# Second block's down product by one level of Strassen's algorithm, with its sums on VectorE

## Chip, core and metric

The kernel runs on one core of one Trainium2 chip, in f32 throughout. The metric is the device time of one execution in microseconds, taken as the median of several runs. A profiled execution of the same program gives the trace; its own time stands beside its span below. The engines are TensorE (PE; PEld are its weight loads), VectorE (DVE), ScalarE (ACT), GpSimd (POOL) and SyncE (SP), which here only issues transfers.

## What is computed

Two transformer blocks one after the other on 512 tokens of width 1024. The first has latent attention, a state-space branch, cross-attention and a mixture of 64 experts; the second has gated mixing, sparse attention and a feed-forward layer. The change is in the last lines of the second block:

```python
D_FF = int(math.ceil(8 * D_MODEL / 3 / 256)) * 256      # 2816
...
        h = rmsnorm(x, norm_ffn_w[l])
        x = x + (jax.nn.silu(h @ w_gate[l]) * (h @ w_up[l])) @ w_down[l]
    return rmsnorm(x, final_norm_w)
```

The down product multiplies activations of 512 x 2816 with weights of 2816 x 1024.

## The kernel before

Each engine has one program, written out by hand in the order in which it runs; engines meet through semaphores that count up (`wait_ge`). The matrix products land in eight PSUM banks of 128 x 512 f32. A fixed list (`psum_order`, line 157) names every bank tile in order, who reads it (act or dve), and the class `Plan` works out which bank it gets and which earlier tile must have been read first (`free`). `OWN_BANKS` (line 108) gives "fd", the down product, its eight banks in turn.

Weights of the dense products come as panels of 128 x 1024 f32 (512 KB) from the array `stream` into `ring`, twelve slots in on-chip memory. `panel_plan` (line 315) lists them in order and says after which event a slot may be filled again; SP issues them in `load_panel` (line 830) and waits there for the event. The weights of the experts come from other arrays, by larger transfers, partly into the same ring.

The stage before the down product computes gate and up, 22 units (`for n in range(UNITS)`, lines 1534 on TensorE, 1964 on ScalarE, 2721 on VectorE). Each unit is already one level of Strassen's algorithm in Winograd's form: seven block products p1 to p7 of four matmuls each (128 x 128 by 128 x 256), in turn over the eight banks (`unit_product`, line 1523, bank (7n + part) mod 8), four sums of weights for each unit on VectorE (`weight_sums`, line 2692, `sums_ready`), and seven additions on VectorE that put the parts together (`unit_read` counts them). After each odd unit VectorE multiplies silu(gate) by up, which makes two of the 22 feature blocks `actf[k]` (128 features x 512 tokens) ready and counts `actf_ready`.

The down product (`down_step`, line 1555) multiplies those blocks with panels of w_down. Half 0 (the first 512 output columns) runs over all 22 blocks with the four token tiles inside, in four banks; half 1 runs tile after tile, each over all 22 blocks. VectorE adds each finished bank to the residual x4. In half 1 it then takes the tile's mean square (`ask_rms`, line 2111), GpSimd raises it to the power -0.5, VectorE scales the tile, and SP stores it.

Of the kernel before, what the change touches and what calls it, by code (L numbers as in the profile page):

```python
# [107 lines left out]
OWN_BANKS = {"s5y": (7,), "s2": (0, 1, 2, 3), "pt2": (4, 5), "o2": (6, 7), "fd": (2, 3, 4, 5, 6, 7, 0, 1)}  # L108
# [48 lines left out]
def psum_order():  # L157
# [151 lines left out]
    for i in range(8):  # L309
        add("fd", i, "dve")  # L310
# [4 lines left out]
def panel_plan():  # L315
# [34 lines left out]
    p += [("fd", k, ("fd", 4 * (k // 11) + 3) if k % 11 == 10 else ("ffn", k - k // 11)) for k in range(FT)]  # L350
# [6 lines left out]
def host_stream(w):  # L357
# [7 lines left out]
    def rows(m, k, c0, n):  # L365
        return m[k * P:(k + 1) * P, c0:c0 + n]

    def two(m, i, c0, n=512):
        out = np.zeros((P, 2, 512), f)
        for b in range(2):  # L370
            out[:, b, :n] = rows(m, 2 * i + b, c0, n)
        return out.reshape(P, 1024)
# [28 lines left out]
    def pair(m, i, n):  # L401
# [18 lines left out]
        "fd": lambda i: two(w["w_down_2"][0], i % 11, 512 * (i // 11)),  # L420
# [102 lines left out]
def build(nc, a, out, scratch):  # L523

    plan = Plan(psum_order(), 8)
    with ExitStack() as ctx:
# [215 lines left out]
        outb = slab1  # L742

# [82 lines left out]
        def _(sp):  # L826
# [3 lines left out]
            def load_panel(n):  # L830

                if n >= RING:
# [3 lines left out]
                    elif n - N1 >= RING:  # L836
# [3 lines left out]
                        elif key[0] == "ffn":  # L840
                            sp.wait_ge(ffn_used, key[1] + 1)
                        else:
# [103 lines left out]
        def _(pe):  # L946
# [608 lines left out]
            def down_step(half, t, k):  # L1555
                return nc.tensor.matmul(tile("fd", 4 * half + t)[:, :], actf[k][:, t * P:(t + 1) * P],  # L1556
                                        panel("fd", 11 * half + k // 2)[:, (k % 2) * 512:(k % 2) * 512 + 512],
                                        start=(k == 0), stop=(k == FT - 1))

            for t in range(NT):  # L1560
                free("fd", t)
            pe.wait_ge(unit_kept, UNITS)
            pe.wait_ge(unit_read, 7 * UNITS - 2)
            for k in range(FT):
                if k % 2 == 0:
                    need("fd", k // 2)
                    pe.wait_ge(actf_ready, k // 2 + 1)
                for t in range(NT):
                    mm = down_step(0, t, k)
                    if k == FT - 1:  # L1570
                        close(mm, "fd", t)
                    elif k % 2 == 1 and t == NT - 1:
                        mm.then_inc(ffn_used, 1)
            for t in range(NT):
                free("fd", 4 + t)
                if t == 0:
                    pe.wait_ge(unit_read, 7 * UNITS)
                for k in range(FT):
# [1407 lines left out]
```

## Time and profile before

| | us |
|---|---|
| median of three runs | 2114.28 |
| lowest and highest | 2112.44, 2119.64 |
| the profiled execution's own time | 2117.95 |
| its span | 2116.1 |
| mean granted TensorE clock | 0.976 of full |

The span runs from the first to the last instruction of the trace; the execution's own time has 1.85 us more around it. Busy time is that of an engine's instructions. TensorE's records overlap, so the mean duration of one is longer than what it costs; its rate is busy time divided by count. Each f32 matmul leaves two records. "Idle before" is time in which an engine stood still just before instructions of the group, with what ended it. A line number can be that of a helper: L1997 is any VectorE addition, subtraction or product of two tensors, L2000 any scaled one.

### The profile page before, as it was taken

Reading aid. Unit: us, or ns where it says so; the run is one execution under the profiler, and the core shown is the slowest. Engines: PE = TensorE matmul, PEld = TensorE weight load, DVE = VectorE, ACT = ScalarE, POOL = GpSimd, SP = SyncE. Lnnn points to the kernel's source line nnn. Section 1 sums busy time; section 2 is a strip of 40 time slices with the busy share of each in tenths; the row PEclk is TensorE's granted clock in tenths of the full one; section 3 lists DMA queues with packets and bytes.
Section 4 is the critical chain, followed back from the end, with each engine's and each line's share of the span. In section 5 each row is a group of like instructions: output and inputs, shape, how many; then the busy total and the mean of one; then the engine's idle time right before and its main releaser. Section 6 shows DMA issues by size and latency. Waiting matters only on the chain.

```text
span 2116.1 us, 26992 instructions
## 1 busy us (share of the span) xinstructions
PE 1955.6 (92%) x10450; PEld 1021.1 (48%) x10450; DVE 891.8 (42%) x1804; ACT 474.3 (22%) x1042; POOL 336.2 (16%) x295
## 2 busy tenths in 40 slices
PE   7897999999997899999989998799988899999997
PEld 3333434444543344443333333344745588888443
DVE  5998691213167323332332234601266555454012
ACT  2233531010121233333323332211236000000000
POOL 0654161000006401101010015300023000000000
PEclk9998999999999999999999999899999999999999
DMA  6116743220415999999999999603310122222200
GB/s 233 50 47 206 208 134 148 80 70 23 159 60 216 316 393 400 400 399 393 386 388 382 388 391 373 240 20 139 140 40 2 40 80 100 80 83 97 80 30 30
DMA packets 74730, 393.68 MB, mean 186 GB/s; under 512 B 12194, under 2 KB 12450, under 8 KB 57760
## 3 DMA queue, kind: packets, MB, share of 16 engines
q1 hardware_dynamic: 45216, 300.95, 37.8%
q10 hardware_dynamic: 16592, 58.01, 8.1%
q0 software_dynamic: 12848, 33.74, 4.4%
q8 instruction: 47, 0.77, 0.2%
q14 instruction: 27, 0.22, 0.0%
HBM read 371.51 MB, written 55.09 MB: 202 GB/s over the span
## 4 chain that ended last, share of the span: by engine, by line
PE 70%; DMA 14%; DVE 9%; issue 4%; POOL 2%; ACT 1%; SPq 0%; POOLq 0%; ACTq 0%; DVEq 0%
PE bank L975 28%; PE bank L1306 13%; PE bank L1531 13%; DMA ring<-w_exp_down 10%; PE bank L1556 6%; PE bank L984 2%; DVE slab L2000 1%; DMA slab<-w_exp_down 1%; DVE work L1994 1%; PE bank L1324 1%; DVE s5x L1997 1%; DMA slab<-x_rows,s5x 1%; DVE slab L1997 1%; PE bank L1382 1%; PE bank L1037 1%
## 5 line engine op out<-in xcount | busy, mean ns | idle before, releaser
L975 PE MATMUL bank<-slab,ring 128*128 128x512 f32 (+1 forms) x784 | 330.1, 581 | 12.0 <-DMA ring<-stream 11.1
L975 PE MATMUL bank<-ring,slab 128*128 128x512 f32 (+1 forms) x608 | 252.8, 577 | 3.7 <-ACT slab L1594 1.9
L2458 DVE COPY slab<-bank 32x512 f32<-32x512 f32 x124 | 80.9, 688 | 410.9 <-PE bank L1314 410.9
L1306 PE MATMUL bank<-ring,slab 128*32 128x512 f32 x1536 | 232.7, 607 | 19.7 <-DMA slab<-w_exp_down 16.4
L1306 PE MATMUL bank<-slab 128*32 128x512 f32 x1536 | 227.9, 597 | 21.9 <-DMA ring<-w_exp_down 14.6
L975 PEld LDWEIGHTS bank<-slab,ring 128*128 128x128 f32 x784 | 149.0, 192 | 188.7 <-issue 187.1
L1314 PE MATMUL bank<-ring,slab 128*32 128x512 f32 x512 | 227.4, 598 | 0.0
L1314 PE MATMUL bank<-slab 128*32 128x512 f32 x480 | 214.4, 600 | 0.0
L975 PEld LDWEIGHTS bank<-ring,slab 128*128 128x128 f32 x608 | 115.7, 191 | 137.3 <-issue 129.5
L2774 POOL TENSOR_TENSOR small<-small 128x1 f32<-128x1 f32 (+2 forms) x30 | 26.6, 888 | 873.9 <-DVE small L1994 873.9
L1556 PE MATMUL bank<-ring,slab 128*128 128x512 f32 x352 | 151.2, 593 | 0.0
L1306 PEld LDWEIGHTS bank<-ring,slab 128*32 128x32 f32 x1536 | 73.1, 112 | 153.3 <-issue 153.2
L1306 PEld LDWEIGHTS bank<-slab 128*32 128x32 f32 x1536 | 71.2, 110 | 152.4 <-issue 145.9
L2849 POOL DMA_INDIRECT slab<-x_rows,s5x x64 | 61.9, 967 | 503.6 <-PE bank L1268 494.4
L1531 PE MATMUL bank<-work,s5x 128*128 128x256 f32 x528 | 117.6, 379 | 0.0
L1997 DVE TENSOR_TENSOR slab<-bank,slab 96x256 f32<-96x256 f32 (+2 forms) x98 | 49.3, 505 | 151.2 <-PE bank L1556 132.7
L1556 PEld LDWEIGHTS bank<-ring,slab 128*128 128x128 f32 x352 | 67.0, 190 | 83.6 <-issue 83.6
L1531 PEld LDWEIGHTS bank<-work,s5x 128*128 128x128 f32 x528 | 100.5, 190 | 13.4
L1997 DVE TENSOR_TENSOR work<-bank,work 128x256 f32<-128x256 f32 (+1 forms) x74 | 33.5, 454 | 164.5 <-PE bank L975 89.9
L1821 ACT ACTIVATE slab<-bank 32x512 f32<-32x512 f32 x124 | 66.6, 584 | 106.9 <-PE bank L1314 106.9
L1777 ACT ACTIVATE slab<-bank 128x384 f32<-128x384 f32 x128 | 55.8, 488 | 141.3 <-DVE slab L2425 120.9
L1531 PE MATMUL bank<-slab,ring 128*128 128x256 f32 x352 | 79.7, 380 | 0.8 <-DVE slab L1994 0.8
(302 smaller groups left out, 2581.8 us busy)
## 6 DMA issues: line engine op xcount, KB each, us to landing
ring<-stream SPq DMA_DIRECT2D x171, 512.0 KB, 4.3
slab<-w_exp_gu SPq DMA_DIRECT2D x32, 2048.0 KB, 25.2
ring<-w_exp_gu SPq DMA_DIRECT2D x32, 2048.0 KB, 23.5
ring<-w_exp_down SPq DMA_DIRECT2D x32, 1024.0 KB, 28.5
slab<-w_exp_down SPq DMA_DIRECT2D x32, 1024.0 KB, 28.0
y_rows<-zeros ACTq DMA_DIRECT2D x1, 24960.0 KB, 127.7
y_rows<-slab ACTq DMA_DIRECT2D x64, 384.0 KB, 10.4
gb<-rows ACTq DMA_DIRECT2D x5, 512.0 KB, 5.3
```

Source lines behind the costliest of these rows:

```text
L975: mm = nc.tensor.matmul(dst, lhs[k], rhs[k], start=(k == 0), stop=(k == len(lhs) - 1))
L984: mm = nc.tensor.transpose(tile(name, i)[0:parts, j * P:(j + 1) * P], x, ident)
L1306: mm = nc.tensor.matmul(g_bank[32 * g:32 * g + 32, :], x[:, k, 32 * g:32 * g + 32], w[:, 512 * k:512 * k + 512], start=(k == 0), stop=(k = ...
L1314: mm = nc.tensor.matmul(bank[2 + 3 * t + half][96:128, :], h[:, c * CAP + 32 * t:c * CAP + 32 * t + 32], d[:, c * D + 512 * half:c * D + 5 ...
L1531: mm = nc.tensor.matmul(unit_bank(n, p), w[:, k * P:(k + 1) * P], x[:, k, :], start=(k == 0), stop=(k == 3))
L1556: return nc.tensor.matmul(tile("fd", 4 * half + t)[:, :], actf[k][:, t * P:(t + 1) * P], panel("fd", 11 * half + k // 2)[:, (k % 2) * 512: ...
L1777: i = nc.scalar.activation(xe[b][:, 4 * j:4 * j + 4, :], bank[j][:, 0:4 * CAP].rearrange("p (k n) -> p k n", n=CAP), ACT.Copy)
L1821: i = nc.scalar.activation(ye[b % 2][0:32, 512 * half:512 * half + 512], bank[2 + half][96:128, :], ACT.Copy)
L1997: return nc.vector.tensor_tensor(out_, x, y, op)
L2458: i = nc.vector.tensor_copy(ye[b % 2][32:64, 512 * half:512 * half + 512], bank[5 + half][96:128, :])
L2774: nc.gpsimd.tensor_tensor(rstd[:, at:at + w], var[:, at:at + w], minus_half[:, 0:w], ALU.pow).then_inc(rstd_ready, 1)
L2849: pool.indirect_dma_start(xg[e % 2][0:CAP, :], None, scratch["x2"], bass.IndirectOffsetOnAxis(ap=slot_tok[:, e:e + 1].bitcast(U32), axis=0 ...
```

## The change

The activations A (512 tokens x 2816 features) and the weights W (2816 x 1024) are each cut into two by two blocks. Tokens are cut into two halves of 256, output columns into two of 512, and features by turns: block row k of the eleven takes `actf[2k]` as the first and `actf[2k+1]` as the second. Seven products replace eight: p1 = A11 W11, p2 = A12 W21, p5 = S1 T1, p6 = S2 T2, p7 = S3 T3, p3 = S4 W22, p4 = A22 T4, where S1 = A21 + A22, S2 = S1 - A11, S3 = A11 - A21, S4 = A12 - S2 are 256 wide and T1 = W12 - W11, T2 = W22 - T1, T3 = W22 - W12, T4 = W21 - T2 are 512 wide. Each product has two token tiles and eleven contraction blocks.

TensorE makes three passes. The first has p1, p2 (plain steps) and, one block behind, p6, p7 (sum steps), in all eight banks. The second has p5 and p3 by turns. The third has p4, tile after tile. VectorE makes the eight sums of each block from the ring during the first pass (`down_sums`); S2, T2, S3 and T3 have two places each, so it waits for `ffn_used` before it writes a third; S1, T1, S4 and T4 are kept for all eleven blocks in memory that is free by then. ScalarE copies p1 out of its banks. VectorE adds the other parts to x4 as they close; tiles 0 and 1 are finished after p3, tiles 2 and 3 after p4.

The panels of w_down are ordered by pairs for each block (W11 with W21, then W12 with W22), and six more panels, "fb", bring W22 a second time for the second pass: 28 in place of 22. A slot that held a "fd" panel is refilled once TensorE has used the block's sums and VectorE has made all eight.

```diff
@@ -105,7 +105,10 @@
-OWN_BANKS = {"s5y": (7,), "s2": (0, 1, 2, 3), "pt2": (4, 5), "o2": (6, 7), "fd": (2, 3, 4, 5, 6, 7, 0, 1)}
+OWN_BANKS = {"s5y": (7,), "s2": (0, 1, 2, 3), "pt2": (4, 5), "o2": (6, 7), "fd": (2, 3, 4, 6, 5, 7, 0, 1)}
+DOWN_PARTS = ("p1", "p2", "p6", "p7", "p5", "p3", "p4")
...
-    for i in range(8):
-        add("fd", i, "dve")
+    for p in DOWN_PARTS:
+        for t in range(2):
+            add("fd", 2 * DOWN_PARTS.index(p) + t, "act" if p == "p1" else "dve")
...
-    p += [("fd", k, ("fd", 4 * (k // 11) + 3) if k % 11 == 10 else ("ffn", k - k // 11)) for k in range(FT)]
+    p += [("fd", i, ("ffn", i // 2)) for i in range(FT)]
+    p += [("fb", i, ("fd", 2 * DOWN_PARTS.index("p3") + 1)) for i in range(FT // 4 + 1)]
...
+        KH = FT // 2
+        def a_block(i, j, k, t):
+            return actf[2 * k + j][:, 256 * i + t * P:256 * i + (t + 1) * P]
+        def s1_at(k):
+            return s5x[:, 256 * k:256 * k + 256]
+        def s4_at(k):
+            return s5x[:, 2816 + 256 * k:3072 + 256 * k] if k < 5 else slab8[:, 512 + 256 * (k - 5):768 + 256 * (k - 5)]
+        def s2_at(k):
+            return s5x[:, 4096 + 512 * (k % 2):4352 + 512 * (k % 2)]
+        def s3_at(k):
+            return s5x[:, 4352 + 512 * (k % 2):4608 + 512 * (k % 2)]
+        def t1_at(k):
+            return slab1[:, 512 * k:512 * k + 512] if k < 8 else work[:, 512 * (k - 8):512 * (k - 7)]
+        def t4_at(k):
+            return work[:, 1536 + 512 * k:2048 + 512 * k] if k < 10 else slab8[:, 0:512]
+        def t2_at(k):
+            return slab9[:, 1024 * (k % 2):1024 * (k % 2) + 512]
+        def t3_at(k):
+            return slab9[:, 1024 * (k % 2) + 512:1024 * (k % 2) + 1024]
+        p1_kept = [gb[:, 512 * t:512 * t + 512] for t in range(2)]
+        u2_kept, u3_kept = [t2_at(1), t2_at(0)], [t3_at(1), t3_at(0)]
...
+                            sp.wait_ge(sums_ready, 4 * UNITS + 8 * key[1] + 8)
...
@@ -1552,34 +1597,59 @@
                 pe.wait_ge(t_ready, 4)
                 unit_product(n, "p4", wb[:, 512:1024], tb4)
 
-            def down_step(half, t, k):
-                return nc.tensor.matmul(tile("fd", 4 * half + t)[:, :], actf[k][:, t * P:(t + 1) * P],
-                                        panel("fd", 11 * half + k // 2)[:, (k % 2) * 512:(k % 2) * 512 + 512],
-                                        start=(k == 0), stop=(k == FT - 1))
-
-            for t in range(NT):
-                free("fd", t)
-            pe.wait_ge(unit_kept, UNITS)
-            pe.wait_ge(unit_read, 7 * UNITS - 2)
-            for k in range(FT):
+            def down_step(p, t, k, x, w):
+                i = 2 * DOWN_PARTS.index(p) + t
+                if k == 0:
+                    free("fd", i)
+                mm = nc.tensor.matmul(tile("fd", i)[:, :], x, w, start=(k == 0), stop=(k == KH - 1))
+                if k == KH - 1:
+                    close(mm, "fd", i)
+                return mm
+
+            def plain_steps(k):
+                need("fd", 2 * k)
+                w = panel("fd", 2 * k)
+                for t in range(2):
+                    if k == 0 and t == 0:
+                        pe.wait_ge(unit_read, 7 * UNITS - 7)
+                    elif k == 0:
+                        pe.wait_ge(unit_kept, UNITS)
+                    down_step("p1", t, k, a_block(0, 0, k, t), w[:, 0:512])
+                if k == 0:
+                    pe.wait_ge(unit_read, 7 * UNITS - 5)
+                for t in range(2):
+                    down_step("p2", t, k, a_block(0, 1, k, t), w[:, 512:1024])
+
+            def sum_steps(k):
+                if k == 0:
+                    pe.wait_ge(unit_read, 7 * UNITS)
+                for p, x, w, n in (("p6", s2_at(k), t2_at(k), 4), ("p7", s3_at(k), t3_at(k), 6)):
+                    pe.wait_ge(sums_ready, 4 * UNITS + 8 * k + n)
+                    for t in range(2):
+                        mm = down_step(p, t, k, x[:, t * P:(t + 1) * P], w)
+                if k < KH - 1:
+                    mm.then_inc(ffn_used, 1)
+
+            pe.wait_ge(actf_ready, KH - 1)
+            for k in range(KH + 1):
+                if k == KH - 1:
+                    pe.wait_ge(actf_ready, KH)
+                if k < KH:
+                    plain_steps(k)
+                if k >= 1:
+                    sum_steps(k - 1)
+            pe.wait_ge(sums_ready, 4 * UNITS + 8 * KH)
+            for k in range(KH):
+                for t in range(2):
+                    down_step("p5", t, k, s1_at(k)[:, t * P:(t + 1) * P], t1_at(k))
                 if k % 2 == 0:
-                    need("fd", k // 2)
-                    pe.wait_ge(actf_ready, k // 2 + 1)
-                for t in range(NT):
-                    mm = down_step(0, t, k)
-                    if k == FT - 1:
-                        close(mm, "fd", t)
-                    elif k % 2 == 1 and t == NT - 1:
-                        mm.then_inc(ffn_used, 1)
-            for t in range(NT):
-                free("fd", 4 + t)
-                if t == 0:
-                    pe.wait_ge(unit_read, 7 * UNITS)
-                for k in range(FT):
-                    if t == 0 and k % 2 == 0:
-                        need("fd", 11 + k // 2)
-                    mm = down_step(1, t, k)
-                close(mm, "fd", 4 + t)
+                    need("fb", k // 2)
+                for t in range(2):
+                    down_step("p3", t, k, s4_at(k)[:, t * P:(t + 1) * P],
+                              panel("fb", k // 2)[:, 512 * (k % 2):512 * (k % 2) + 512])
+            for t in range(2):
+                for k in range(KH):
+                    down_step("p4", t, k, a_block(1, 1, k, t), t4_at(k))
@@ -1970,6 +2040,8 @@
+            for t in range(2):
+                copy("fd", t, p1_kept[t], tile("fd", t)[:, :])
@@ -2746,18 +2818,88 @@
                     tt(x, x, unit_out(n - 1), ALU.mult).then_inc(actf_ready, 1)
                 if n + 2 < UNITS:
                     weight_sums(n + 2)
-            for half in range(2):
-                for t in range(NT):
-                    i = 4 * half + t
-                    full("fd", i)
-                    x = tm(x4, t)[:, half * 512:half * 512 + 512]
-                    tt(x, tile("fd", i)[:, :], x, ALU.add).then_inc(dve_evac, 1)
-                    if half == 1:
-                        dve.wait_ge(dve_evac, plan.done("fd", i))
-                        ask_rms(tm(x4, t), 4 + t)
-                        r, n = pending[4 + t]
-                        dve.wait_ge(rstd_ready, n)
-                        stt(tm(outb, t), tm(x4, t), r, gb[:, D:2 * D], ALU.mult, ALU.mult).then_inc(norm_ready, 1)
+            dve.wait_ge(unit_part, 7 * UNITS)
+            dve.wait_ge(unit_read, 7 * UNITS)
+            dve.wait_ge(actf_ready, KH)
+
+            def down_sums(k):
+                for h in range(2):
+                    at = panel_at["fd", 2 * k + h]
+                    dve.wait_ge(landed[slot(at)], 16 * uses(at))
+                if k >= 2:
+                    dve.wait_ge(ffn_used, k - 1)
+                left, right = panel("fd", 2 * k), panel("fd", 2 * k + 1)
+                w11, w21, w12, w22 = left[:, 0:512], left[:, 512:1024], right[:, 0:512], right[:, 512:1024]
+                a11, a12, a21, a22 = [actf[2 * k + j][:, 256 * i:256 * i + 256] for i in range(2) for j in range(2)]
+                done = 4 * UNITS + 8 * k
+                tt(s1_at(k), a21, a22, ALU.add).then_inc(sums_ready, 1)
+                tt(t1_at(k), w12, w11, ALU.subtract).then_inc(sums_ready, 1)
+                dve.wait_ge(sums_ready, done + 1)
+                tt(s2_at(k), s1_at(k), a11, ALU.subtract).then_inc(sums_ready, 1)
+                dve.wait_ge(sums_ready, done + 2)
+                tt(t2_at(k), w22, t1_at(k), ALU.subtract).then_inc(sums_ready, 1)
+                tt(s3_at(k), a11, a21, ALU.subtract).then_inc(sums_ready, 1)
+                tt(t3_at(k), w22, w12, ALU.subtract).then_inc(sums_ready, 1)
+                dve.wait_ge(sums_ready, done + 3)
+                tt(s4_at(k), a12, s2_at(k), ALU.subtract).then_inc(sums_ready, 1)
+                dve.wait_ge(sums_ready, done + 4)
+                tt(t4_at(k), w21, t2_at(k), ALU.subtract).then_inc(sums_ready, 1)
+
+            for k in range(KH):
+                down_sums(k)
+
+            def x_block(i, j, t):
+                return tm(x4, 2 * i + t)[:, 512 * j:512 * j + 512]
+
+            def part(p, t):
+                i = 2 * DOWN_PARTS.index(p) + t
+                full("fd", i)
+                return tile("fd", i)[:, :]
+
+            def read(p, t):
+                dve.wait_ge(dve_evac, plan.done("fd", 2 * DOWN_PARTS.index(p) + t))
+
+            for t in range(2):
+                x = x_block(0, 0, t)
+                y = part("p2", t)
+                tt(x, y, x, ALU.add).then_inc(dve_evac, 1)
+                dve.wait_ge(act_evac, plan.done("fd", t))
+                read("p2", t)
+                tt(x, x, p1_kept[t], ALU.add).then_inc(unit_read, 1)
+            for t in range(2):
+                tt(u2_kept[t], part("p6", t), p1_kept[t], ALU.add).then_inc(dve_evac, 1)
+                read("p6", t)
+                x = x_block(0, 1, t)
+                tt(x, x, u2_kept[t], ALU.add).then_inc(unit_read, 1)
+            for t in range(2):
+                tt(u3_kept[t], part("p7", t), u2_kept[t], ALU.add).then_inc(dve_evac, 1)
+                read("p7", t)
+                for j in range(2):
+                    x = x_block(1, j, t)
+                    tt(x, x, u3_kept[t], ALU.add).then_inc(unit_read, 1)
+            dve.wait_ge(unit_read, 7 * UNITS + 8)
+            for t in range(2):
+                y = part("p5", t)
+                x = x_block(0, 1, t)
+                tt(x, y, x, ALU.add)
+                x = x_block(1, 1, t)
+                tt(x, y, x, ALU.add).then_inc(dve_evac, 1)
+
+            def finish_tile(t):
+                r, n = pending[4 + t]
+                dve.wait_ge(rstd_ready, n)
+                stt(tm(outb, t), tm(x4, t), r, gb[:, D:2 * D], ALU.mult, ALU.mult).then_inc(norm_ready, 1)
+
+            for p, i, j, first in (("p3", 0, 1, 0), ("p4", 1, 0, 2)):
+                for t in range(2):
+                    if t == 0:
+                        read("p5" if p == "p3" else "p3", 1)
+                    y = part(p, t)
+                    x = x_block(i, j, t)
+                    tt(x, y, x, ALU.add).then_inc(dve_evac, 1)
+                    read(p, t)
+                    ask_rms(tm(x4, first + t), 4 + first + t)
+                    finish_tile(first + t)
```

## Rows read from the trace of the kernel before

**Rows 1.** The page, busy time, share of the span and instructions of each engine.

```profile
PE 1955.6 (92%) x10450; PEld 1021.1 (48%) x10450; DVE 891.8 (42%) x1804; ACT 474.3 (22%) x1042; POOL 336.2 (16%) x295
```

**Rows 2.** Stretches: length, busy us (instructions) of five engines, PEclk, DMA share, GB/s.

```profile
700.00:1310.00 610.00, 565.55 (x5620) 240.01 (x5615) 185.69 (x441) 189.97 (x434) 85.98 (x89) 0.99 0.99 386
1685.00:1951.00 266.00, 265.92 (x1232) 234.61 (x1233) 135.46 (x255) 20.23 (x34) 0.00 (x0) 1.00 0.24 84
1951.00:2102.30 151.30, 151.29 (x354) 66.87 (x352) 15.95 (x27) 0.00 (x0) 1.65 (x3) 1.00 0.17 52
2102.30:2116.10 13.80, 0.00 (x0) 0.00 (x0) 3.85 (x7) 0.00 (x0) 0.55 (x1) 0.62 0.09 38
```

**Rows 3.** The chain that ended last: start us, us, engine and line, its end.

```profile
1685.08 266.14 PE bank L1531 x1232
1951.23 132.20 PE bank L1556 x308
2086.77 18.30 issue
2105.69 1.28 DVE slab L2000
```

**Rows 4.** Groups, 1951 us to the end: busy us, mean ns, idle before, releaser.

```profile
L1556 PE MATMUL bank<-ring,slab 128*128 128x512 f32 x352 | 151.2, 593 | 0.0
L1556 PEld LDWEIGHTS bank<-ring,slab 128*128 128x128 f32 x352 | 67.0, 190 | 83.6 <-issue 83.6
L1997 DVE TENSOR_TENSOR slab<-bank,slab 128x512 f32<-128x512 f32 x8 | 5.5, 692 | 132.7 <-PE bank L1556 132.7
```

**Rows 5.** VectorE's groups in the gate and up stage.

```profile
L1997 DVE TENSOR_TENSOR slab<-bank,work 128x256 f32<-128x256 f32 x87 | 36.8, 424 | 53.6 <-PE bank L1531 51.3
L1997 DVE TENSOR_TENSOR s5x<-ring 128x512 f32<-128x512 f32 x44 | 30.1, 684 | 0.0
...
L1997 DVE TENSOR_TENSOR s5x<-s5x,ring 128x512 f32<-128x512 f32 x22 | 15.2, 691 | 0.7
```

**Rows 6.** Timeline, one unit's four weight sums: start us, us, then what it is.

```profile
1928.70 0.68 DVE L1997 TENSOR_TENSOR s5x<-ring 128x512 f32<-128x512 f32 x1
...
1929.41 0.69 DVE L1997 TENSOR_TENSOR s5x<-s5x,ring 128x512 f32<-128x512 f32 x1
1930.02 0.68 DVE L1997 TENSOR_TENSOR s5x<-ring 128x512 f32<-128x512 f32 x1
...
1930.62 0.68 DVE L1997 TENSOR_TENSOR s5x<-ring,s5x 128x512 f32<-128x512 f32 x1
```

**Rows 7.** Timeline, hand-over from gate and up to the down product.

```profile
1951.07 24.20 PE L1556 MATMUL bank<-ring,slab 128*128 128x512 f32 x56
1951.27 0.42 DVE L1997 TENSOR_TENSOR slab<-bank,work 128x256 f32<-128x256 f32 x1 [1.30 <-PE bank L1531]
...
1951.73 1.23 DVE L1997 TENSOR_TENSOR slab<-slab 128x1024 f32<-128x1024 f32 x1
```

**Rows 8.** Panel loads from 1900 us with us to landing, and SP's waits.

```profile
ring<-stream SPq DMA_DIRECT2D x20, 512.0 KB, 3.4
...
SPq L844 <- PE bank L1556: 64.7, 10, 6.5
```

**Rows 9.** Timeline, the last tile on VectorE.

```profile
2102.33 0.69 DVE L1997 TENSOR_TENSOR slab<-bank,slab 128x512 f32<-128x512 f32 x1 [14.24 <-PE bank L1556]
...
2105.69 1.28 DVE L2000 SCALAR_TENSOR_TENSOR slab<-slab,small,gb 128x1024 f32<-128x1024 f32 x1 [0.66 <-POOL small L2774]
```

**Rows 10.** Stretches around an idle time of TensorE, columns as in rows 2.

```profile
1357.00:1368.00 11.00, 0.81 (x2) 0.00 (x0) 10.13 (x14) 4.78 (x7) 5.81 (x5) 0.71 0.83 319
1370.00:1373.00 3.00, 2.12 (x10) 2.13 (x11) 0.00 (x0) 1.63 (x3) 0.00 (x0) 0.50 1.03 410
```

More of the change, by code:

```diff
@@ L371, in two, with b22_pair @@
             out[:, b, :n] = rows(m, 2 * i + b, c0, n)
+        return out.reshape(P, 1024)
+    def b22_pair(m, i):
+        out = np.zeros((P, 2, 512), f)
+        for b in range(2):
+            if 2 * i + b < FT // 2:
+                out[:, b] = rows(m, 2 * (2 * i + b) + 1, 512, 512)
         return out.reshape(P, 1024)
@@ L419, in host_stream @@
         "fu": lambda i: a_panel(w["w_up_2"][0], i * P),
-        "fd": lambda i: two(w["w_down_2"][0], i % 11, 512 * (i // 11)),
+        "fd": lambda i: two(w["w_down_2"][0], i // 2, 512 * (i % 2)),
+        "fb": lambda i: b22_pair(w["w_down_2"][0], i),
     }
```

## Prediction

> **What bounds the kernel now.** I read the page first: TensorE is busy 92% of the span, VectorE 42% [rows 1]. A share over the whole span says little about one stage, so the second view is the table of stretches [rows 2]. From 700 to 1310 us the experts' weights stream in with the transfer engines full (share 0.99) and TensorE nearly full as well. From 1685 to 1951 us the gate and up products run, from 1951.0 to 2102.3 us the down product that the change rewrites, and in both TensorE is busy all the time at a granted clock of 1.00. The last 13.8 us belong to the last tile's way out. The chain of what ended last says the same: 266.1 us of gate and up, then 132.2 us of the down product, then what is called issue, then the last VectorE step [rows 3]. So in this stage every microsecond of TensorE work is a microsecond of the span, and VectorE has room: in the grouped view of 1951 us to the end it has eight additions from a bank and waits 132.7 us for TensorE before them [rows 4].
>
> **What the change takes from TensorE.** Before, 176 matmuls of 128x128 by 128x512 (22 feature blocks, 4 token tiles, 2 halves), shown as 352 records, because each f32 matmul leaves two. They take 151.2 us with no idle time before any [rows 4], so one record costs 151.2/352 = 0.4295 us and one matmul 0.859 us. The records' own mean of 593 ns is longer since neighbours overlap; the sum goes by the rate. After, seven block products of 11 contraction blocks and 2 token tiles are 154 matmuls of the same shape. 22 fewer x 0.859 = 18.9 us. Nothing else is taken off: the 154 still cost 132.3 us.
>
> The Trainium skill, "TensorE: Matmul & The Clock Gate", section "Back-to-back issue gap", has a rule that would make this smaller: it gives 131 ns as the sustained spacing of 512-column matmuls and says that N/2.4 + 2.5 ns (about 216 ns) counts too much. With two passes for each record (an estimate, from the four passes of true FP32 in "FP8 and Floating Point Precision", section "TensorE Precision Notes") the page's 131 ns would make a matmul 0.52 us and the saving 11.5 us. The trace has 0.4295 us for a record, twice 215 ns, and so bears out the formula that the page calls too high; the row decides.
>
> **Do waits and many banks slow the matmuls that are left?** The first pass goes over eight banks for each contraction block, with a wait before p6 and before p7. No row shows such a down product, but the gate and up stage is built alike: seven products of eight matmul records each, in turn over eight banks, a wait or two before each, VectorE making sums beside it. Its 1232 records take 266.1 us [rows 3], 0.216 us for 256 columns, half of 0.4295 plus 1 ns. I take nothing for the waits. If each of the 22 waits before sums cost 0.1 us, it were 2 us.
>
> **What is added on VectorE, first pass.** For each of the 11 blocks eight sums: four 512 wide and four 256 wide, SBUF to SBUF. The 512 wide ones have rows, 0.684 and 0.691 us. A 256 wide one from SBUF has none; the nearest is the 256 wide one with a bank as source, 0.424 us; below it bound half of 0.684, 0.34 us, above it the full 0.69 us [rows 5]. I take 0.424, since the width is the same. A block costs 4 x 0.69 + 4 x 0.42 = 4.5 us (4.1 to 5.5), all eleven 49 us (45 to 61). The dependent sums of a unit start 0.60 to 0.71 us apart [rows 6], so the waits on its own semaphore cost nothing beside the durations. TensorE takes 8 x 0.859 = 6.87 us for a block. VectorE is the faster, at 65% (at most 80%) of the time.
>
> **The hand-over into the down product.** TensorE starts down matmuls at 1951.07 us. VectorE reads the last unit's bank at 1951.27 and multiplies gate and up from 1951.73, 1.23 us, to 1952.96 [rows 7]. Only behind that stand the first sums: S1, T1, S2, T2, 2.2 us, done about 1955.3; S3 and T3 about 1956.4. TensorE meanwhile has the plain products of blocks 0 and 1, eight matmuls, and wants p6 at 1951.07 + 6.87 = 1957.9 and p7 1.7 us later. Slack 2.6 and 3.2 us. If the cover were gone, the whole 4.2 us to 1955.3 would be waited for. The first banks are free earlier than in the old order, but as no idle time stands before the old first matmul, that wins nothing.
>
> **Behind the waits.** From block 2 on VectorE waits until the sums of two blocks before have been used (ffn_used), behind which its whole queue stands. It gets 10.3 us from there to the next p6 and needs 2.2; for the last block 6.87 us, since no plain step is left. After the eleventh block's sums (about 2020.9) it adds p2, 2 to 3 us, before TensorE asks for banks 4 and 6 for p3 at 1951.07 + 90 x 0.859 = 2028.4. ScalarE copies p1 in that time, on an otherwise empty queue. p4 wants the banks of p6 at 2064. All are hidden by several microseconds; what is next late is nothing but TensorE itself.
>
> **Transfers.** 28 panels in place of 22, six more of 512 KB. A panel lands 3.4 us after its issue, and SP today waits for TensorE, not the reverse [rows 8]. A pair is asked for when its slot's block is used, six blocks or 41 us ahead of need. The added wait on sums_ready holds SP's queue, but sums are done before the matmuls that use them. The last refill (freed when block 7 is used, about 2009) comes before the first output transfer, so output rows don't queue behind panels. Cost 0.
>
> **The end.** Before, the last addition starts at 2102.33 and the last scaling at 2105.69 [rows 9]; one tile needs 4.7 us on VectorE and GpSimd. After, p3 closes tiles 0 and 1 at 19.8 and 18.9 us before TensorE's end. VectorE's p5 additions end at about -18.7, tile 0 at -14.0, tile 1 at -9.4; p4 closes tile 2 at -9.45, done -4.7, and tile 3 finds VectorE idle. Slack 4.7 us; the 13.8 us of the tail stay.
>
> **Sum.** -18.9 + 0 + 0 + 0. The profiled execution took 2117.95 us for a span of 2116.1, so it would become 2099.1, with a span of 2097.2. It lay 3.67 us above the median of the three timed runs, 2114.28; against that median the forecast is 2114.28 - 18.9 = 2095.4.
>
> **Rivals.**
> *VectorE becomes the bound of the first pass.* If every step of the sums waited for the last one's write to end and the durations came out at some 0.94 us a sum, a block would take 7.5 us, and TensorE would idle (7.5 - 6.87) x 11 = 7 us: 2102.4. For it: chained sums, alternately dependent. Against it: the spacing in [rows 6] and the 65% above.
>
> *The gain is eaten in the expert stage.* The stream array grows by six panels and moves the arrays behind it in memory. The 610 us stage with its transfers at 0.99 share [rows 2] has nothing to spare; 2% there is 12 us, which would leave 2107 to 2109, within 0.3% of before. Nothing in the trace speaks for it but the spread of the timed runs, 2112.44 to 2119.64.
>
> *The clock falls, slower than before.* If TensorE had small gaps between the groups and lost the full clock in the first pass, its 75.6 us would take up to 75.6 us more: 2171. It decides from 18.9 us of full-speed work done at half speed, a quarter of the pass. The trace shows such a place: after 11 us with 0.8 us of TensorE work the next stretch runs at 0.50, 1.2 of 2.4 GHz [rows 10]. Against it: in the gate and up stage, with the same turning of banks, 1.00 throughout [rows 2]. The Trainium skill has this as a rule, same page, section "A second HAM failure mode: psum-queue depth-cycling": cycling through banks makes short idle times in which the clock swings. By that rule this rival would hold; the trace's bank-cycling stage does not agree.
>
> **Chances and range.** Forecast 0.84; VectorE as bound 0.07; eaten in the expert stage 0.06; clock 0.03. A measurement of this kernel can tell about 0.3%, 6.3 us. The first two are faster by more: 0.91. The third is the same: 0.06. The fourth is slower: 0.03. The range takes the timed runs' spread less 18.9 (2093.5 to 2100.7), 3 us for where the arrays lie (0.5% of the expert stage), and, upwards, 2 us for waits or the seven of the first rival: 2090 to 2104.
>
> **What would show it.** In the profile after: the down product's line with 308 records in 132.3 us and no idle time before it; granted clock 1.00 there; VectorE at 45 to 61 us of sums in the first 75.6 us; the tail unchanged at 13.8 us; the stretches before 1951 us as they are. Wrong if p6 or p7 wait for VectorE in each round (first rival), if the start of the gate and up stage has moved (second), or if records stretch past 0.43 us (third).

## Result and the profile after

| | before | after |
|---|---|---|
| median, first comparison (4 runs each) | 2116.96 | 2090.95 |
| lowest and highest | 2112.44, 2124.89 | 2090.05, 2097.74 |
| the profiled execution's own time | 2117.95 | 2090.72 |
| its span | 2116.1 | 2088.9 |

The ratio is 0.9889, with a 95% interval of 0.9864 to 0.9915: faster by 1.1%. Two later comparisons, each on another chip, gave 0.9916 [0.9887, 0.9944] and 0.9912 [0.9895, 0.9929]. The forecast of 2095.4 against 2114.28 is a ratio of 0.9911, inside the first interval. The kernel before has a fourth run here, of 2124.89 us, so its median lies above the 2114.28 that the forecast started from.

The page first, then the end of the chain that ended last (start us, us, what), which answers to [rows 1] and [rows 3]:

```profile
PE 1931.3 (92%) x10406; PEld 1008.5 (48%) x10406; DVE 941.8 (45%) x1906; ACT 475.1 (23%) x1044; POOL 333.4 (16%) x295
```

```profile
1676.75 266.14 PE bank L1576 x1232
1942.89 122.76 PE bank L1604 x286
2069.07 8.78 issue
```

VectorE gained 50 us of work, and TensorE's share stayed at 92%. The gate and up stage takes 266.14 us as before. It also begins 8.3 us earlier (1676.75 against 1685.08), though nothing ahead of it was edited. The clean measure of the change is therefore the stretch from there to the end of the span, less 266.14: before 2116.1 - 1685.08 - 266.14 = 164.9 us, after 2088.9 - 1676.75 - 266.14 = 146.0 us. That is 18.9 us, the whole of what was forecast. It is called the down stretch below.

Stretches of it (columns as in [rows 2]): the three passes and the tail.

```profile
1942.70:2018.30 75.60, 75.60 (x178) 33.48 (x178) 48.68 (x98) 1.19 (x2) 0.00 (x0) 1.00 0.36 125
2018.30:2056.10 37.80, 37.80 (x90) 16.75 (x89) 6.49 (x11) 0.00 (x0) 0.00 (x0) 1.00 0.00 0
2056.10:2075.00 18.90, 18.90 (x45) 8.10 (x43) 11.54 (x22) 0.00 (x0) 1.65 (x3) 1.00 0.21 83
2075.00:2088.90 13.90, 0.08 (x1) 0.00 (x0) 3.84 (x7) 0.00 (x0) 0.55 (x1) 0.69 0.09 38
```

TensorE is busy in every microsecond of the three passes at a granted clock of 1.00, where [rows 2] had 151.3 us of the same. The passes last 75.6, 37.8 and 18.9 us. VectorE is busy for 48.7 of the first 75.6 us, with 88 sums and ten other instructions. Who waited for whom in the stretch (us in total, times, longest):

```profile
PEld bank L1604 <- issue: 72.9, 305, 0.2
DVE slab L2069 <- PE bank L1604: 37.3, 4, 31.2
DVE s5x L2069 <- PE bank L1604: 25.2, 9, 3.0
...
PEld bank L1604 <- DVE s5x L2069: 0.2, 1, 0.2
```

VectorE waits for TensorE, in the first pass 25.2 us. TensorE's weight loads waited for VectorE for 0.2 us, once; that is shorter than the running matmul and cost nothing.

The hand-over, timeline (start us, us, what), which answers to [rows 7]:

```profile
1942.73 7.03 PE L1604 MATMUL bank<-ring,slab 128*128 128x512 f32 x16
...
1943.39 1.23 DVE L2069 TENSOR_TENSOR slab<-slab 128x1024 f32<-128x1024 f32 x1
...
1944.81 0.42 DVE L2069 TENSOR_TENSOR s5x<-slab 128x256 f32<-128x256 f32 x1 [0.19 <-DVE slab L2069]
...
1945.75 0.42 DVE L2069 TENSOR_TENSOR s5x<-s5x,slab 128x256 f32<-128x256 f32 x1
1946.09 0.69 DVE L2069 TENSOR_TENSOR slab<-ring,slab 128x512 f32<-128x512 f32 x1
...
1948.56 0.42 DVE L2069 TENSOR_TENSOR s5x<-slab 128x256 f32<-128x256 f32 x1
...
1949.60 3.60 PE L1604 MATMUL bank<-slab,s5x 128*128 128x512 f32 x8
```

The multiplication of gate and up runs from 1943.39 us, S1 starts at 1944.81, T2 at 1946.09, and it is written by 1946.8. The eight sums of block 0 start 0.34 or 0.60 us apart and those of block 1 begin at 1948.56, 3.75 us behind. The matmul group that begins with p6 starts at 1949.60, right behind the sixteen records of two plain blocks.

### The profile page after: what moved, and what is told of

Read it like the earlier page. It is cut to its first block, busy times and chain, and to the rows that moved or that the text cites. A ratio compares the mean times of both kernels' runs of the same rounds, so it can differ in the third digit from the quotient of the medians.

```text
span 2088.9 us, 27041 instructions
## 1 busy us (share of the span) xinstructions
PE 1931.3 (92%) x10406; PEld 1008.5 (48%) x10406; DVE 941.8 (45%) x1906; ACT 475.1 (23%) x1044; POOL 333.4 (16%) x295
## 4 chain that ended last, share of the span: by engine, by line
PE 71%; DMA 13%; DVE 9%; issue 3%; POOL 1%; ACT 1%; DVEq 0%; SPq 0%; POOLq 0%; ACTq 0%
PE bank L1020 29%; PE bank L1351 13%; PE bank L1576 13%; DMA ring<-w_exp_down 12%; PE bank L1604 6%; PE bank L1029 2%; DVE slab L2072 2%; PE bank L1369 1%; DVE work L2066 1%; DVE s5x L2069 1%; DVE slab L2069 1%; PE bank L1082 1%; PE bank L1427 1%; DVE slab L2066 1%; PE bank L1313 1%
## 5 line engine op out<-in xcount | busy, mean ns | idle before, releaser
L1020 PEld LDWEIGHTS bank<-slab,ring 128*128 128x128 f32 x784 | 148.4, 191 | 188.5 <-issue 186.9
L1020 PEld LDWEIGHTS bank<-ring,slab 128*128 128x128 f32 x608 | 115.5, 191 | 137.7 <-issue 129.7
L2069 DVE TENSOR_TENSOR slab<-bank,work 128x256 f32<-128x256 f32 (+1 forms) x96 | 42.6, 444 | 84.6 <-PE bank L1576 52.6
L1576 PEld LDWEIGHTS bank<-slab,ring 128*128 128x128 f32 x352 | 66.8, 190 | 10.1 <-DVE slab L2066 1.0
```

Source lines behind the costliest of these rows:

```text
L1020: mm = nc.tensor.matmul(dst, lhs[k], rhs[k], start=(k == 0), stop=(k == len(lhs) - 1))
L1576: mm = nc.tensor.matmul(unit_bank(n, p), w[:, k * P:(k + 1) * P], x[:, k, :], start=(k == 0), stop=(k == 3))
L2069: return nc.vector.tensor_tensor(out_, x, y, op)
```

## The experiments

**The changed kernel again, on a second chip.**

> The changed kernel once more, against the kernel before on the same chip, to size the whole gain. Theory A (the down product alone gained, 18.9 us; the 8.3 us by which the gate and up stage began earlier in the profiled execution belong to the expert stage's own scatter): median 16 to 23 us below before. Theory B (something of the change also speeds up what lies ahead of it, by some 5 to 8 us): 24 to 28 us below, with the gate and up stage starting 5 us or more earlier in each profile.

Median 2095.83 (six runs) against 2112.72 (nineteen): 16.9 us. Its gate and up stage began at 1678.61 us and its span ended at 2090.8, so its down stretch is 146.05 us. That is theory A in the medians and in the stretch. The gate and up stage starts 6.5 us earlier than in the first profile of before, though, which is what theory B asked of each profile; the next runs bear on that.

**Does the longer stream array help the experts?** The kernel before, with six more panels that nobody reads:

```diff
-    out = np.empty((len(PANELS), P, PW_), f)
+    out = np.zeros((len(PANELS) + 6, P, PW_), f)
```

> The kernel before with six unused panels at the end of the stream array, so that the arrays behind it, the experts' weights among them, lie 3 MB further on in memory, as in the changed kernel. Nothing else differs. Theory A: same as before within 0.15% (3 us). Theory B (memory placement speeds up the expert stage): 5 to 8 us faster, the gate and up stage starting that much earlier.

Ratio 1.0001 [0.9979, 1.0022], medians 2113.45 and 2112.72. The chain of its profile:

```profile
1679.71 266.14 PE bank L1531 x1232
1945.86 132.20 PE bank L1556 x308
```

Here the gate and up stage of an unchanged kernel also starts 5.4 us earlier than in the first profile of it, and the time didn't improve. Its down stretch is 2110.7 - 1679.71 - 266.14 = 164.9 us, that of the first profile. The interval leaves room for a gain of at most 0.2% (some 4 us), less than the 5 to 8 us of theory B.

**The changed kernel with the old layout of memory.**

```diff
+                src = a["stream"][n] if PANELS[n][0] != "fb" else a["stream_b"][PANELS[n][1]]
-                sp.dma_start(ring[:, slot(n) * PW_:(slot(n) + 1) * PW_], a["stream"][n]).then_inc(landed[slot(n)], 16)
+                sp.dma_start(ring[:, slot(n) * PW_:(slot(n) + 1) * PW_], src).then_inc(landed[slot(n)], 16)
```

> The changed kernel with its six extra panels in an array of their own, declared last, so that the stream array and all behind it have the sizes and the order of the kernel before. Theory A: as the changed kernel, 16 to 23 us below before. Theory B by placement: the 5 to 8 us ahead of the down product are lost again, 19 us below before where the changed kernel shows 25 or more.

Ratio 0.9920 [0.9890, 0.9949], median 2098.43, 14.3 us below before; the changed kernel beside it 0.9916. The chain:

```profile
1684.45 266.14 PE bank L1577 x1232
```

The median lies 1.7 us under the 16 to 23 us of theory A, and 2.6 us above the changed kernel's, both within the intervals. So it missed its forecast by a little, and its interval is too wide to tell. Its profile has the gate and up stage at 1684.45 us, and the down stretch is 2096.6 - 1684.45 - 266.14 = 146.0 us. This profile alone would look like theory B, the padded one speaks against it, and of the medians it is the padded kernel's that rules out an effect of placement of 5 us or more.

**The saved matmuls alone.** The kernel before, with 21 matmuls left out and nothing added (the first tile of half 1 gets only its last feature block):

```diff
                 for k in range(FT):
...
+                    if t == 0 and k < FT - 1:
+                        continue
...
```

> The kernel before with 21 of the 176 matmuls of the down product left out (the first tile of half 1 takes only its last feature block; the product is left out otherwise), so it has the saved TensorE work without sums, extra panels or new order. If a matmul on this path is worth 0.859 us and nothing else counts: 18.0 us below before. If the sums, waits and panels of the changed kernel cost nothing, its down stage is only 0.9 us shorter than this one's. A rival in which part of the gain is given back (VectorE, waits) has this one ahead of the changed kernel by more than 1 us.

Median 2095.77 (seven runs) against 2112.72, 17.0 us; ratio 0.9921 [0.9893, 0.9949]. The chain:

```profile
1675.94 266.14 PE bank L1531 x1232
1942.09 75.53 PE bank L1556 x176
2017.62 38.64 PE bank L1583 x90
```

Down stretch 2089.0 - 1675.94 - 266.14 = 146.9 us: 18.0 us less than before for 21 matmuls, 0.857 us each. The changed kernel has 146.0, which is the twenty-second matmul. So 88 sums, 22 waits, six more panels and a new order of 154 matmuls together cost less than 0.1 us.

**VectorE loaded twice.** This kernel and the next three were executed once each, and are judged by their profiles alone. Behind each sum a useless one of the same width:

```diff
                 tt(s1_at(k), a21, a22, ALU.add).then_inc(sums_ready, 1)
+                waste(256)
                 tt(t1_at(k), w12, w11, ALU.subtract).then_inc(sums_ready, 1)
+                waste(512)
...
```

> The changed kernel with a useless sum of the same width behind each of VectorE's eight sums of a block (into tables no longer needed; 8 x 11 more instructions). In the changed kernel a block's sums take 3.75 us from start to start, so here 7.5 us, against TensorE's 6.87 us. From the first down matmul to the end of the span the changed kernel takes 146.0 us. Theory A (the sums cost nothing until they are longer than TensorE's block, then only the excess counts): first pass ends when eleven blocks of 7.5 us are done, about 9 to 10 us later, 155 to 156 us, TensorE waiting for VectorE before p6 or p7 in the later blocks and not in the first ones. Theory B (VectorE's work beside the matmuls slows them in proportion): records of more than 0.43 us from the first block on, and more than 156 us.

Span 2097.4, gate and up from 1673.98 us, down stretch 157.3 us: 11.3 us longer. TensorE's waits for VectorE, then four groups of the timeline, then stretches of it:

```profile
PEld bank L1604 <- DVE slab L2069: 17.8, 17, 4.5
PE bank L1604 <- DVE slab L2069: 5.1, 8, 3.6
```

```profile
1939.96 7.03 PE L1604 MATMUL bank<-ring,slab 128*128 128x512 f32 x16
...
2012.83 3.86 PE L1604 MATMUL bank<-slab,s5x 128*128 128x512 f32 x8 [0.21 <-DVE slab L2069]
2020.33 8.34 PE L1604 MATMUL bank<-slab,s5x 128*128 128x512 f32 x12 [3.64 <-DVE slab L2069]
...
2028.51 1.88 PE L1604 MATMUL bank<-ring,s5x 128*128 128x512 f32 x4
```

```profile
1940.00:1955.00 15.00, 15.00 (x37) 6.64 (x36) 14.61 (x30) 0.00 (x0) 0.00 (x0) 1.00 0.42 141
2012.00:2018.00 6.00, 4.48 (x10) 1.35 (x8) 6.00 (x14) 0.00 (x0) 0.00 (x0) 1.00 0.00 0
2018.00:2022.00 4.00, 1.67 (x2) 0.84 (x3) 4.00 (x10) 0.00 (x0) 0.00 (x0) 0.68 0.00 0
2022.00:2026.00 4.00, 4.00 (x6) 1.69 (x5) 3.90 (x9) 0.00 (x0) 0.00 (x0) 0.50 0.00 0
2026.00:2030.00 4.00, 4.00 (x10) 1.72 (x9) 3.83 (x8) 0.00 (x0) 0.00 (x0) 0.97 0.00 0
```

The first 15 us are as before, TensorE busy throughout; the records keep their pace, sixteen of them in 7.03 us as in the changed kernel. From the middle of the pass p6 of the next block comes 7.50 us after the last (2012.83, 2020.33), which is VectorE's block. Theory A's mechanism holds: TensorE waits in the later blocks and not in the first ones. Theory B's time (more than 156 us) came out and its mechanism didn't, since no record is longer at the start.

1.3 us more were lost than theory A's upper figure, and the timeline says where. The last p6 starts at 2020.33, 80.4 us behind the first matmul of the pass at 1939.96. In the changed kernel 168 records lie between the two, 72.1 us. So VectorE's pace cost 8.3 us, of which 3.64 are the last wait: the last block has no plain step in front. Then comes the clock. Behind that standstill the stretches from 2018 to 2026 us show 0.68 and 0.50, where 0.50 is 1.2 GHz. The twelve records from 2020.33 us, eight of sum steps and four of p5, take 8.2 us to the start of the next at 2028.51, where their price is 5.2: 3.0 us. The two together are the 11.3 us.

**VectorE loaded three times.**

> As before, with two useless sums behind each: 11.25 us a block. Theory A: the first pass lasts as long as VectorE's 124 us, about 51 us longer than in the changed kernel, 197 us from the first down matmul to the end, slower than the kernel before (164.9). On the clock: each round TensorE then idles some 4.4 us of 11.25, in several pieces. If turning through eight banks with such gaps takes the clock away, the granted clock of the first pass falls well under 1.00 and its matmuls cost up to 0.86 us a record; as TensorE isn't the bound there, the time would still be about 197 as long as a block's eight matmuls stay under 11.25 us (13.7 at half clock: 224 us).

Span 2139.7, gate and up from 1677.60, down stretch 196.0 us, against 197 expected; in the one timed run 2141.55 us where the kernel before had 2107.42. The rival "VectorE becomes the bound", driven beyond its point, is slower than before. Its stretches, TensorE's waits, and three groups behind a pause:

```profile
1943.60:2070.00 126.40, 90.30 (x181) 35.34 (x179) 126.00 (x267) 1.19 (x2) 0.00 (x0) 0.92 0.21 75
1984.00:1990.00 6.00, 5.88 (x10) 2.17 (x11) 6.00 (x13) 0.00 (x0) 0.00 (x0) 0.72 0.00 0
2018.00:2029.00 11.00, 7.15 (x17) 2.63 (x16) 11.00 (x25) 0.00 (x0) 0.00 (x0) 1.00 0.26 95
```

```profile
PEld bank L1604 <- DVE slab L2069: 55.5, 23, 7.3
```

```profile
1983.98 5.64 PE L1604 MATMUL bank<-slab,s5x 128*128 128x512 f32 x8 [3.02 <-DVE slab L2069]
...
2017.72 1.99 PE L1604 MATMUL bank<-slab,s5x 128*128 128x512 f32 x4 [3.02 <-DVE slab L2069]
...
2062.72 7.61 PE L1604 MATMUL bank<-slab,s5x 128*128 128x512 f32 x12 [6.45 <-DVE slab L2069]
```

The granted clock of the whole first pass is 0.92. From the second round on TensorE stands still for 2.2 to 3.0 us at once, and for 6.45 us before the last p6. After one such pause (before 1983.98 us) the stretch from 1984 to 1990 us shows 0.72, after another (before 2017.72 us) that from 2018 to 2029 us shows 1.00. In the rounds this costs nothing, since VectorE sets the pace. Behind the last pause it does: twelve records take 7.61 us, where their price is 5.2.

**Without the block of lag.** Each block's sum steps directly behind its plain steps:

```diff
-            for k in range(KH + 1):
+            for k in range(KH):
...
-                if k < KH:
-                    plain_steps(k)
-                if k >= 1:
-                    sum_steps(k - 1)
+                plain_steps(k)
+                sum_steps(k)
```

> The changed kernel with each block's sum steps directly behind its plain steps, so that only block 0's plain steps cover the hand-over. By the changed kernel's trace T2 of block 0 is ready 4.05 us after the first down matmul, and p6 is wanted after 3.43 us. Theory A: one wait of 0.6 to 0.8 us before the first p6, none later, 146.7 us from the first down matmul to the end. Theory B (each block's sums come late when the lag is gone): a wait in every block, 150 us or more.

Span 2090.8, gate and up from 1677.88, down stretch 146.8 us, 0.8 more. The hand-over:

```profile
1943.86 3.60 PE L1604 MATMUL bank<-ring,slab 128*128 128x512 f32 x8
...
1947.21 0.69 DVE L2067 TENSOR_TENSOR slab<-ring,slab 128x512 f32<-128x512 f32 x1
...
1948.00 3.67 PE L1604 MATMUL bank<-slab,s5x 128*128 128x512 f32 x8 [0.55 <-issue]
```

p6 starts 4.14 us behind the first matmul, where eight records cost 3.43: 0.7 us, of which 0.55 show as idle. T2, started at 1947.21, was just written. No gap follows it. The lag's worth is this hand-over and nothing else.

**Less work ahead of the end.** The changed kernel without ten matmuls of p4's first tile:

```diff
                 for k in range(KH):
+                    if t == 0 and k < KH - 1:
+                        continue
...
```

> The changed kernel without ten of the eleven matmuls of p4's first tile, 8.6 us of TensorE's work just ahead of the end (that much of the product is left out). Theory A (TensorE bounds this stage only as long as VectorE's finishing of tiles is covered, with 4.7 us to spare): VectorE still finishes tile 2 where it did, and the last tile's addition comes at once behind it, so only 4.7 us are won: 141.3 us from the first down matmul to the end. Theory B (every matmul is worth its 0.859 us here too): 137.4 us.

Span 2081.6, gate and up from 1674.62, down stretch 140.8 us. 8.6 us of TensorE's work were taken away, 5.2 us came out, 0.5 more than expected. The additions that open tiles 1, 2 and 3 on VectorE:

```profile
2058.68 0.68 DVE L2076 TENSOR_TENSOR slab<-bank,slab 128x512 f32<-128x512 f32 x1
...
2063.23 0.69 DVE L2076 TENSOR_TENSOR slab<-bank,slab 128x512 f32<-128x512 f32 x1
...
2067.79 0.68 DVE L2076 TENSOR_TENSOR slab<-bank,slab 128x512 f32<-128x512 f32 x1
```

They follow each other 4.55 us apart with no wait between, one tile after the other: VectorE is the bound of this end once TensorE's cover is some 5 us shorter. Theory A. The larger part of the 0.5 us beyond the forecast is slack that the 4.7 us before the last tile leave out: in the changed kernel VectorE waited 0.30 us before tile 2 as well.

**A shorter way out for the last tile.** The statistics of its second half are taken before p4's last bank closes, and it is scaled and stored in two halves:

```diff
+                    if first + t == NT - 1:
+                        link(nc.vector.bn_stats(stats[:, 6:12], x_block(1, 1, t)))
                     y = part(p, t)
...
+                        for h in range(2):
+                            c = slice(512 * h, 512 * h + 512)
+                            stt(tm(outb, NT - 1)[:, c], tm(x4, NT - 1)[:, c], r, gb[:, D + 512 * h:D + 512 * h + 512], ALU.mult, ALU.mult).then_inc(norm_ready, 1)
```

> The changed kernel with a shorter way out for the last tile: the statistics of its second 512 columns, which are final after p5, are taken before p4's last bank closes, and it is scaled and stored in two halves. Off the path behind the last matmul come one 0.6 us statistics step, and perhaps part of the transfer (512 KB took 2.6 us). From the first down matmul to the end of the span: 145.2 to 145.5 us if only the statistics count, 144.9 or less if the halves overlap too, against 146.0; in the medians nothing that can be told from the changed kernel (under 0.05%).

Span 2091.9, gate and up from 1680.29, down stretch 145.5 us: 0.5 to 0.6 us won. On VectorE:

```profile
2073.85 0.69 DVE L2901 BATCH_NORM_STATS2 small<-slab 128x6 f32<-128x512 f32 x1
...
2079.45 0.69 DVE L2911 BATCH_NORM_STATS2 small<-slab 128x6 f32<-128x512 f32 x1
...
2081.50 1.42 DVE L2075 SCALAR_TENSOR_TENSOR slab<-slab,small,gb 128x512 f32<-128x512 f32 x2 [0.67 <-POOL small L2933]
```

The statistics at 2073.85 lie under the last matmuls; behind them stands one at 2079.45 in place of the two that the changed kernel has there (2075.84 and 2076.45, shown below under the end). The two halves brought nothing that shows. Median 2095.43 against 2114.95, ratio 0.9907 [0.9890, 0.9925]; beside it the changed kernel again:

> The changed kernel again, beside the version above and the kernel before on the same chip. If the gain is the down product's alone, its median is 16 to 22 us below before, and the stretch from the first down matmul to the end is 146.0 us again, wherever the gate and up stage starts; if something ahead of it gained too, more than 24 us.

Median 2097.27, 17.7 us below before, ratio 0.9912; gate and up from 1680.33, span 2092.5, down stretch 146.0 us. The shorter tail beats it in the profile, by 0.5 to 0.6 us; the medians can't tell it from the changed kernel.

## Why the forecast held, step by step

**TensorE's bound and the price of a matmul.** Right, and the step that carries all: 22 x 0.859 = 18.9 us, and the down stretch shrank by 18.9 (164.9 to 146.0) in each of four profiles of the changed kernel or its relaid form, within 0.1 us. The 21 left out by hand gave 18.0. The spacing for 512 columns that the Trainium skill gives as sustained ("TensorE: Matmul & The Clock Gate", "Back-to-back issue gap"), from which the prediction estimated a saving of 11.5 us, isn't borne out.

**Waits and eight banks cost nothing.** Right: no idle time before any of the 308 records but the overlapped 0.2 us, and granted clock 1.00. The bound of 2 us for the waits was not needed.

**VectorE's sums.** The mechanism right, the size off: 4.5 us a block was forecast, 3.75 measured. For eleven blocks that is 41.3 us, below the 45 to 61 that the prediction named as its sign. VectorE's 48.7 us of busy time in the first pass look like the forecast 49 only by chance, as ten other instructions are in them. I added durations (0.42 and 0.69 us), but the next instruction starts 0.34 or 0.60 us after the last one started; [rows 6] had shown the 0.60 already. The lower bound of 4.1 us was too high for the same reason. The Trainium skill, "VectorE: DVE Perf Modes", section "The TRN2 errata — SBUF-src ops pay a fixed extra latency per instruction", has two formulas for such an instruction of N columns: 58 + N cycles at 0.96 GHz, an estimate of 0.33 and 0.59 us here, and (N + 151)/0.96, 0.42 and 0.69 us. The trace agrees with both, with the first in the spacing of starts (0.34 and 0.60 us) and with the second in the durations. In this queue the spacing was the price.

**The hand-over.** T2 ready 4.2 us behind the first matmul was forecast, 4.05 came out; covered by two plain blocks of 6.87. Without the lag the uncovered part was 0.8 us. The 4.2 us that I put down for a lost cover assumed that no plain step stands in front at all.

**Behind the waits.** Right. VectorE waited for used sums nine times, 3.0 us at the longest, and TensorE never had to wait for what stood behind these waits. VectorE had read p2 by 2014.1 us, 5.9 us before p3's first matmul at 2019.98 us.

**Transfers.** No matmul waited for a panel. SP's waits in the last stage:

```profile
SPq L889 <- PE bank L1604: 46.4, 8, 6.0
...
SPq L886 <- DVE work L2069: 4.9, 1, 4.9
```

SP waits for TensorE 46.4 us. The added wait on `sums_ready` (L886) is on record once, with 4.9 us; the wait on `ffn_used` just ahead of it in the queue was fulfilled only by the sum steps of block 0, later than that block's sums, so it is doubtful that the added one held anything. No panel was late.

**The end.** Tail 13.9 us, as before. In the timeline of the last tile, [4.73] is the time that VectorE was idle before its addition, the slack of 4.7 us that was forecast:

```profile
2075.12 0.69 DVE L2069 TENSOR_TENSOR slab<-bank,slab 128x512 f32<-128x512 f32 x1 [4.73 <-PE bank L1604]
2075.84 0.69 DVE L2160 BATCH_NORM_STATS2 small<-slab 128x6 f32<-128x512 f32 x1
2076.45 0.68 DVE L2161 BATCH_NORM_STATS2 small<-slab 128x6 f32<-128x512 f32 x1
...
2078.47 1.28 DVE L2072 SCALAR_TENSOR_TENSOR slab<-slab,small,gb 128x1024 f32<-128x1024 f32 x1 [0.66 <-POOL small L2916]
```

The shortened p4 showed what happens beyond it.

**The sum and the level.** 2095.4 was forecast against a median of 2114.28. The first comparison gave 2090.95, 26.0 us below before, of which 18.9 are accounted for. It lies just above 2090, the lower end of the range, and that it lies inside is partly luck: the 7 us beyond the forecast come from no step of the prediction. The 7 us left belong to where the gate and up stage began. In the twelve profiles it began at 1685.1 and 1679.7 us (before, padded), 1675.9 (fewer matmuls), 1676.8, 1678.6, 1680.3 and 1684.5 (changed, relaid), and from 1674.0 to 1680.3 in the other five, with the same instructions ahead of it. The scatter arises mostly in the expert stage: its first matmul lies between 683.0 and 685.3 us in all, its last between 1295.9 and 1307.9. With nineteen runs of before (2107.98 to 2122.74) the difference of the medians is 16.9 us, with eleven on a third chip 17.7. So I put the excess of the first comparison down to scatter of that stage; what makes it scatter between executions stays open.

The range has a flaw of its own: its terms upwards, 2 us or the seven of the first rival on 2100.7, and 3 us for placement, lead past its upper end of 2104. The measurement came nowhere near that end.

**The rivals.** VectorE as the bound: not so in the change; forced, at 7.5 us a block, it cost 11.3 us and not the 7 I priced. My price counted (7.5 - 6.87) for each block and left out that the last block has no plain step before it (8.3 us up to the last p6), and the clock that falls in the gap (3.0 us). Gain eaten in the expert stage by placement: no effect seen (1.0001). The sign that I named for it, a moved start of the gate and up stage, did appear, 8.3 us and in the other direction. It is no sign: the start moves as much between kernels that are the same up to there. The clock: 1.00 throughout. It does fall once TensorE stands still for 3.6 us, as the doubled sums show, but turning through eight banks doesn't make such gaps. The Trainium skill ("TensorE: Matmul & The Clock Gate", section "A second HAM failure mode: psum-queue depth-cycling") tells of a kernel whose turning through banks left short idle times in which the clock swung. This trace doesn't agree: no idle time and 1.00 in all three passes.

## What to carry to other kernels

Where one engine is busy in every microsecond of a stage, a cut of its work is worth exactly its own duration, provided that the work moved to another engine fits under what is left: here 3.75 us of sums under 6.87 us of matmuls, with a block of lag for the hand-over. Price a queue of short VectorE instructions by the spacing of their starts, not by their durations. And when a stage ahead of the change scatters by more than the change is worth, compare the stretch from a fixed landmark behind it to the end, which here repeated within 0.1 us while whole times spread over 15.

## What the hardware showed that was not expected

Around a pause of TensorE of 3.64 us stretches show 0.68 and 0.50 of the clock, some 7 us at the lower level, though the engine had run at 1.00 until then; pauses of 3.02 us in the threefold kernel were followed by 0.72 in some cases and by 1.00 in others. A shorter one of 2.17 us, before 1995.22 us, was followed by 0.72 as well, so the length of the pause alone doesn't decide it. Which of them take the clock away stays open.

In the kernel with doubled sums, VectorE's records grow in the course of the pass, the 256 wide ones from 0.42 to 0.49 us and the 512 wide ones from 0.69 to 0.76, while their starts stay 0.34 and 0.60 us apart. In the threefold kernel, whose pass is longer, they reach 0.54 and 0.81. I have no explanation.
